# Narrower output products and one copy per four heads in the dilated attention of a decoder trunk

## The chip, the cores and the metric

The kernel runs on one core of one Trainium2 chip. The metric is the device time of one execution in microseconds (us), median of several runs. In the rows, PE is TensorE's matrix multiplication and PEld its weight load, DVE is VectorE, ACT is ScalarE, SP is SyncE; a name with q behind it (ACTq, PEldq) is that engine's queue or sequencer.

## The reference, cut to what matters

The program is one step of a two-layer trunk: a gated DeltaNet layer with its MLP, then a dilated attention layer with its MLP, for 1,024 prompt tokens and 8 sample tokens. The change touches the attention of the prompt tokens alone:

```python
HEADS_B = 8; KV_HEADS_B = 2; GQA_B = 4; HEAD_DIM_B = 64; N_BRANCH = 3
...
        kg = jnp.take(k_ext, kidx, axis=1).astype(jnp.float32)
        vg = jnp.take(v_ext, kidx, axis=1).astype(jnp.float32)
        s = jnp.einsum('nqhgd,nqkhd->nqhgk', q_blk.astype(jnp.float32), kg) * scale + bias
...
        p = jnp.exp(s - lse)
        o = jnp.einsum('nqhgk,nqkhd->nqhgd', p, vg)
```

Eight query heads share two key/value heads ("groups"), four each; a value row has 64 columns for each group. Three branches (dilations 1, 4 and 16) are computed apart and merged by their softmax denominators. In the einsum for `o`, a head needs the 64 value columns of its own group and no others.

## The kernel before, in words

Each engine has its own hand-written instruction stream; the order of the work is the order of the code in it, and the engines meet through counting semaphores (`bank4_free`, `bank4_full`, `probs_ready`, `out_taken` and so on). After the query and key/value projections and the attention of the samples come the 24 prompt tiles: three branches of 8 tiles of 128 queries. `tiles_of` (line 375) walks the tiles on every engine and calls that engine's `step(cur, nxt)`, so the scores of the next tile are made between the parts of the current one. A tile sees nk = 1 or 2 blocks of 128 keys: branch 0 has one tile with nk = 1 and seven with nk = 2; branch 1 has nk = 1 and nk = 2 by turns; branch 2 has nk = 1 throughout. A tile's eight heads are worked in two halves (hs = 0 and 1).

- PE, `step` at line 2170: `turn(cur, 0)` transposes the probabilities of four heads into bank 4 and 5 (line 1770, in `transposes`); `scores(nxt)` makes the next tile's scores in banks 0 to 3 (L2142); then `turn(cur, 1)`, `apply(cur, 0)`, `apply(cur, 1)`. `apply` is the output product (L2165): for each of four heads and each key block, the weights are the transposed probabilities (128x128, f32) and the moving operand is the key block's 128 value columns, both groups. So a head's result takes 128 columns of bank 6 or 7, and half of them, those of the other group, are never read.
- DVE, `step`: `turned` copies transposed probabilities from bank 5 to SBUF (L1630), `biased` adds the bias to the scores (L1612), `maxima` takes the row maxima (L1619, L1622), and `outputs` (L1634 to 1644) copies the softmax statistics and then, for each half, the wanted 64 columns of each head into `o_out`: one copy for each group of a half, 128x128 elements each, four in a tile.
- ACT, `step`: the exponentials (L848), the copy of bank 4 when nk = 2 (L862), and, behind `out_taken`, two DMA issues that store the tile's `o_out` (L881).

In the f32 products here each `matmul` of the code shows as two records in the trace, each with its own weight load. The 560 records of L2165 are 280 products: 8 for each of 13 tiles with nk = 1, and 16 for each of 11 with nk = 2. After the tiles the branches are merged (DVE L1698, L1704), and the output projection and the last MLP follow, long streams of matmuls at L1743 to L1745.

Of the kernel before, what the change touches and what calls it, by code (L numbers as in the profile page):

```python
# [23 lines left out]
P = 128  # L24
# [12 lines left out]
HD = 64  # L37
# [51 lines left out]
        "relu_square_ready": 12, "u_hi_ready": 12},  # L89
# [85 lines left out]
def build(nc, t):  # L175
# [4 lines left out]
    def sem(name):  # L180
        if name not in made:
            made[name] = ctx.enter_context(nc.semaphore(name))
        return made[name]
# [3 lines left out]
    def at(name, shape, dt, where=None, word=4):  # L187

        size = int(np.prod(shape[1:])) * word
        if where is None:  # L190
            place = offset[0]
            offset[0] += -(-size // 32) * 32
        else:
            place = where[0]
            where[0] += -(-size // 32) * 32
            assert where[0] <= where[1], (name, where)
        return nc.alloc_sbuf_tensor_at(name, list(shape), dt, offset=place)
# [101 lines left out]
    v_keys = at("v_keys", [P, BRANCH, CH, P], F32, a)  # L299
    q_tile = at("q_tile", [P, 2, 4, P], F32, a)  # L300
    prob = at("prob", [P, 2, 8, 2 * P], F32, a)
    prob_t = at("prob_t", [P, 2, 8, P], F32, a)
    bias = at("bias", [P, 8, 2 * P], F32, a)
    o_out = at("o_out", [P, 2, OW], F32, a)
# [23 lines left out]
    psum = ctx.enter_context(nc.psum_tensor("psum", [P, 8, HALF], F32))  # L328
# [574 lines left out]
    def _(dve):  # L903
        L = Lane(dve, sem, room=["out0_stored", "out1_stored", "head_output_stored", "state_stored"])
        v = dve
# [608 lines left out]
        def attention_layer():  # L1514
            stored = [0, 0]
            for gi in range(5):
# [4 lines left out]
                for n in range(3 * tiles):  # L1521
# [5 lines left out]
                    third, tile = divmod(n, tiles)  # L1527
                    b = gi - 2 if gi > 1 else 2 * gi + tile // 2
                    d = DIL[b]
                    w = prompt_width(third)  # L1530

                    def by_class(ap):

                        return ap.rearrange("p (r i) -> p i r", r=d)[:, prompt(third, d)]
                    bank = psum[:, TAKES[n % 6]]
                    src = bank[:, 0:w].rearrange("p (i r) -> p i r", r=d)
                    scale = rs[:, prompt(third)].rearrange("p (i r) -> p i r", r=d)
                    mark = "dve_order" if third == 2 else "product_free"
                    v.wait_ge(sem("product_full"), L.next("product_full"))
                    if gi < 2 and tile % 2 == 0:  # L1540
                        for g in range(2):
                            rows = slice(g * HD, (g + 1) * HD)
                            done = v.tensor_tensor(by_class(k_mask[rows, b, g]), src[rows], scale[rows], ALU.mult)
# [89 lines left out]
            def outputs(par):  # L1633

                v.wait_ge(sem(f"out{par}_stored"), L.next(f"out{par}_stored", 32))
                v.tensor_copy(o_out[:, par, 8 * HD:], stats[:, par].rearrange("p m s -> p (m s)")
                ).then_inc(sem("dve_order"), L.add("dve_order"))
                for hs in range(2):
                    v.wait_ge(sem(f"bank{6 + hs}_full"), L.next(f"bank{6 + hs}_full"))
                    for g in range(2):  # L1640
                        dst = o_out[:, par, 0:8 * HD].rearrange("p (g j d) -> p g j d", g=2, j=4)[:, g, 2 * hs:2 * hs + 2]
                        src = psum[:, 6 + hs].rearrange("p (j g c) -> p g j c", g=2, c=P)[:, g, :, g * HD:(g + 1) * HD]
                        mark = ("bank6_free", "out_taken")[hs] if g else "dve_order"
                        v.tensor_copy(dst, src).then_inc(sem(mark), L.add(mark))

            def step(cur, nxt):
                if nxt and (cur is None or nxt[0] != cur[0]):
                    bias_of(nxt[0])
                if cur:
                    turned(cur[3], 0)  # L1650
                if nxt:
                    v.wait_ge(sem(L.last), L.value(L.last))
                    biased(nxt, 0)
                    maxima(nxt, 0)
                    biased(nxt, 1)
                if cur:
                    turned(cur[3], 1)
                if nxt:
                    maxima(nxt, 1)
                if cur:  # L1660
                    outputs(cur[2])
# [10 lines left out]
            for b in range(BRANCH):  # L1672
                mark = "share_args_ready" if b == 2 else "dve_order"
# [16 lines left out]
            with L.loop(CH // 2, "dve merge") as i:  # L1690
                for par in range(2):
# [3 lines left out]
                    for b in range(BRANCH):  # L1695
                        w = share[:, 3, bass.ds(2 * i + par, 1), b].rearrange("p u (j g) -> p (u j) g", g=2)
                        mark = "merge_free" if b == 2 else "dve_order"
# [3 lines left out]
                        if b:  # L1701
                            v.wait_ge(sem(L.last), L.value(L.last))
                            mark = "merged_ready" if b == 2 else "dve_order"
# [27 lines left out]
    def _(pe):  # L1731
        L = Lane(pe, sem, room=["product_free", "out_taken"] + [f"bank{b}_free" for b in range(8)])
        mm = nc.tensor.matmul
# [120 lines left out]
        for h in range(2):  # L1854
            pe.wait_ge(sem(f"bank{6 + h}_free"), L.next(f"bank{6 + h}_free"))
            for k in range(KT):
                done = mm(psum[0:2 * HEADS, 6 + h], w_ab[:, k], x[:, k, halves[h]], start=k == 0, stop=k == KT - 1)
# [3 lines left out]
        for k in range(KT):  # L1861
            done = mm(psum[0:2 * HEADS, 5, 0:NS], w_ab[:, k], s_x[:, k], start=k == 0, stop=k == KT - 1)
# [225 lines left out]
        def attention_layer():  # L2088
            for gi in range(5):
# [3 lines left out]
                for n in range(3 * tiles):  # L2093
                    third, tile = divmod(n, tiles)
# [11 lines left out]
            for b in range(BRANCH):  # L2106
                done = mm(psum[0:NS, 4, b * P:(b + 1) * P], s_kv[:, 2 * b + 1], ident[:], start=True, stop=True)
# [3 lines left out]
            for n in range(NS):  # L2111
# [3 lines left out]
                for b, first, last in ((0, 0, SA), (1, SA, SA + 65), (2, SA + 65, SA + 82), (0, SA + 82, SK)):  # L2115
                    done = mm(psum[0:8, k, lo + first:lo + last], s_qz[:, b, n], s_keys[:, n, first:last],
                              start=True, stop=True)
# [3 lines left out]
            for bank, first, last in ((4, 0, SA), (5, SA, SK)):  # L2121
                pe.wait_ge(sem("bank5_free" if bank == 5 else "s_vrow_ready"), L.next("bank5_free" if bank == 5 else "s_vrow_ready"))
                for n in range(NS):
                    done = nc.tensor.transpose(psum[0:last - first, bank, 8 * n:8 * n + 8], s_p[:, n, first:last],
                                               ident[0:8, 0:8])
# [5 lines left out]
            for n in range(NS):  # L2131
                mm(psum[:, 6, 8 * n:8 * n + 8], s_va[:, n], s_pt[:, 0, 8 * n:8 * n + 8], start=True, stop=False)
                done = mm(psum[:, 6, 8 * n:8 * n + 8], s_vb[:, n], s_pt[0:SB, 1, 8 * n:8 * n + 8], start=False, stop=True)
# [20 lines left out]
            def apply(tile_, hs):  # L2154

                b, tile, par, nk, _ = tile_
                for kt in range(2 - nk, 2):
                    if hs == 1:
                        pe.wait_ge(sem(f"bank{4 + kt}_free"), L.next(f"bank{4 + kt}_free"))
                        L.skip(f"bank{4 + kt}_free", -1)  # L2160
                free = ("bank6_free", "out_taken")[hs]
                pe.wait_ge(sem(free), L.next(free))
                for n in range(4):
                    for kt in range(2 - nk, 2):
                        done = mm(psum[:, 6 + hs, n * P:(n + 1) * P], prob_t[:, kt, 4 * hs + n],  # L2165
                                  v_keys[:, b, bass.ds(tile + kt - 1, 1)].rearrange("p u n -> p (u n)"),
                                  start=kt == 2 - nk, stop=kt == 1)
                done.then_inc(sem(f"bank{6 + hs}_full"), L.add(f"bank{6 + hs}_full"))

            def step(cur, nxt):  # L2170
                if cur:
                    turn(cur, 0)
                if nxt:
                    scores(nxt)
                if cur:
                    turn(cur, 1)
                    apply(cur, 0)
                    apply(cur, 1)
# [150 lines left out]
```

## Time and profile before

| | |
|---|---|
| median of 3 runs | 3120.02 us (3119.8 to 3121.54) |
| the profiled execution's own time | 3127.17 us |
| its span, first to last instruction | 3125.2 us |
| mean granted TensorE clock | 0.949 of 2.4 GHz |
| PE / PEld / DVE / ACT busy over the span | 91% / 89% / 54% / 27% |
| prompt tiles of the attention | about 2080 to 2272 us from the span's start |
| branch 0 / 1 / 2 among them | 2080 to 2152 / 2152 to 2218 / 2218 to 2272 us |
| merge after them | about 2272 to 2325 us |

The profiled execution took 7.15 us more than the median of the runs, so sums are made against its 3127.17 us and their difference is then carried to 3120.02 us. The span is 1.97 us shorter than the execution's own time. Busy shares are averages over stages with different limits: the projections and MLPs are a solid stream on PE, while in the attention the engines hand work to each other.

### The profile page before, as it was taken

Reading aid. Unit: us, or ns where it says so; the run is one execution under the profiler, and the core shown is the slowest. Engines: PE = TensorE matmul, PEld = TensorE weight load, DVE = VectorE, ACT = ScalarE, POOL = GpSimd, SP = SyncE. Lnnn points to the kernel's source line nnn. Section 1 sums busy time; section 2 is a strip of 40 time slices with the busy share of each in tenths; the row PEclk is TensorE's granted clock in tenths of the full one; section 3 lists DMA queues with packets and bytes.
Section 4 is the critical chain, followed back from the end, with each engine's and each line's share of the span. In section 5 each row is a group of like instructions: output and inputs, shape, how many; then the busy total and the mean of one; then the engine's idle time right before and its main releaser. Section 6 shows DMA issues by size and latency. Waiting matters only on the chain. (4 is left out here: it accounts for less than half of the span.)

```text
span 3125.2 us, 47548 instructions
## 1 busy us (share of the span) xinstructions
PE 2853.7 (91%) x18652; PEld 2779.4 (89%) x18652; DVE 1680.2 (54%) x3140; ACT 858.5 (27%) x1907; POOL 0.2 (0%) x4
## 2 busy tenths in 40 slices
PE   5999999999776999999999999758839999999998
PEld 2999999999746999999999999658739999999997
DVE  4766677766344544444444553247867444444445
ACT  3544444444112311221111321025514111122111
POOL 0000000000000000000000000000000000000000
PEclk8999999999757999999999999869969999999999
DMA  3100111102113111111111113731231111111111
GB/s 112 55 17 28 29 35 36 36 16 82 61 47 106 41 54 41 54 40 44 50 40 51 44 55 102 47 90 55 79 117 41 54 41 40 54 40 54 40 41 55
DMA packets 102203, 165.99 MB, mean 53 GB/s; under 512 B 47081, under 2 KB 65809, under 8 KB 101604
## 3 DMA queue, kind: packets, MB, share of 16 engines
q1 hardware_dynamic: 59604, 142.35, 14.3%
q10 hardware_dynamic: 42464, 21.74, 3.5%
q8 instruction: 98, 1.61, 0.2%
q14 instruction: 37, 0.30, 0.0%
HBM read 134.63 MB, written 34.67 MB: 54 GB/s over the span
## 5 line engine op out<-in xcount | busy, mean ns | idle before, releaser
L1743 PE MATMUL psum<-x_hi,w_hi 128*128 128x352 f32 (+1 forms) x2128 | 685.5, 322 | 13.8 <-DVE w_lo L914 7.0
L1744 PE MATMUL psum<-x_lo,w_hi 128*128 128x352 f32 (+1 forms) x2128 | 680.9, 320 | 0.0
L1745 PE MATMUL psum<-x_hi,w_lo 128*128 128x352 f32 (+1 forms) x2128 | 677.7, 318 | 0.0
L1743 PE MATMUL psum<-u_hi,w_hi 128*128 128x352 f32 (+1 forms) x1632 | 524.8, 322 | 2.4 <-DVE u_lo L1717 2.4
L1744 PE MATMUL psum<-u_lo,w_hi 128*128 128x352 f32 (+1 forms) x1632 | 522.2, 320 | 0.0
L1745 PE MATMUL psum<-u_hi,w_lo 128*128 128x352 f32 (+1 forms) x1632 | 520.6, 319 | 0.0
L1743 PEld LDWEIGHTS psum<-x_hi,w_hi 128*128 128x128 f32 x2128 | 400.3, 188 | 17.8 <-DVE x L1432 8.7
L1744 PEld LDWEIGHTS psum<-x_lo,w_hi 128*128 128x128 f32 x2128 | 400.9, 188 | 0.7
L1745 PEld LDWEIGHTS psum<-x_hi,w_lo 128*128 128x128 f32 x2128 | 400.5, 188 | 0.0
L776 ACT ACTIVATE u_hi<-relu 128x352 fp32r<-128x352 f32 (+1 forms) x192 | 94.4, 492 | 1044.1 <-DVE relu L1463 1044.1
L1432 DVE TENSOR_TENSOR x<-x,psum 128x352 f32<-128x352 f32 x336 | 170.6, 511 | 363.7 <-PE psum L1745 363.7
L500 ACT ACTIVATE w_hi<-w_raw,gains 128x512 fp32r<-128x512 f32 x384 | 249.2, 712 | 241.0 <-DMA w_raw<-in_w 132.4
L1743 PEld LDWEIGHTS psum<-u_hi,w_hi 128*128 128x128 f32 x1632 | 307.2, 188 | 3.2 <-issue 2.8
L1744 PEld LDWEIGHTS psum<-u_lo,w_hi 128*128 128x128 f32 x1632 | 307.7, 189 | 0.4
L1745 PEld LDWEIGHTS psum<-u_hi,w_lo 128*128 128x128 f32 x1632 | 307.0, 188 | 0.0
L914 DVE SCALAR_TENSOR_TENSOR w_lo<-w_raw,gains,w_hi 128x512 fp32r<-128x512 f32 x384 | 263.9, 745 | 39.5 <-ACT w_hi L500 39.2
L1845 PE MATMUL psum<-x_hi,w_hi 128*128 128x352 f32 (+1 forms) x768 | 273.0, 355 | 12.8 <-issue 10.3
L1846 PE MATMUL psum<-x_lo,w_hi 128*128 128x352 f32 (+1 forms) x768 | 247.7, 323 | 0.0
L1847 PE MATMUL psum<-x_hi,w_lo 128*128 128x352 f32 (+1 forms) x768 | 247.2, 322 | 0.0
L1460 DVE SCALAR_TENSOR_TENSOR relu<-psum,rs 128x352 f32<-128x352 f32 (+1 forms) x192 | 99.1, 516 | 221.6 <-PE psum L1745 216.8
L1845 PEld LDWEIGHTS psum<-x_hi,w_hi 128*128 128x128 f32 x768 | 147.4, 192 | 13.2 <-issue 10.3
L1466 DVE TENSOR_TENSOR u_lo<-relu,u_hi 128x352 fp32r<-128x352 f32 (+1 forms) x192 | 99.2, 517 | 107.1 <-ACT u_hi L776 107.1
(296 smaller groups left out, 3539.1 us busy)
## 6 DMA issues: line engine op xcount, KB each, us to landing
w_raw<-in_w SPq DMA_DIRECT2D x192, 512.0 KB, 3.7
scratch_att<-o_out ACTq DMA_DIRECT2D x48, 132.0 KB, 2.6
q_tile<-scratch_q SPq DMA_DIRECT2D x24, 256.0 KB, 3.0
merge<-scratch_att SPq DMA_DIRECT2D x8, 768.0 KB, 4.7
scratch_q<-q_stage ACTq DMA_DIRECT2D x24, 176.0 KB, 2.2
x<-in_x SPq DMA_DIRECT2D x8, 516.0 KB, 7.6
scratch_o_heads<-head_out ACTq DMA_DIRECT2D x8, 512.0 KB, 2.7
s_state<-in_s_rec_in ACTq DMA_DIRECT2D x2, 2048.0 KB, 10.0
```

Of the source, the lines that this page charges most:

```text
L500: done = act.activation(w_hi[:, slot, 2 * part + k], w_raw[:, part, k], ACT.Copy, scale=gains[:, bass.ds(unit * UW + 2 * part + k, 1)])
L776: act.activation(u_hi[:, tile, THIRDS[third]], relu[:, 0:width(third)], ACT.Copy).then_inc(sem("u_hi_ready"), L.add("u_hi_ready"))
L914: done = v.scalar_tensor_tensor(w_lo[:, slot, 2 * part + k], w_raw[:, part, k], gains[:, bass.ds(unit * UW + 2 * part + k, 1)], f(w_hi[:, ...
L1432: v.tensor_tensor(out, out, psum[:, TAKES[n % 6], 0:width(third)], ALU.add).then_inc(sem("product_free"), L.add("product_free"))
L1460: v.scalar_tensor_tensor(r, psum[:, TAKES[n % 6], 0:width(third)], 0.0, rs[:, cols], ALU.max, ALU.mult).then_inc(sem("product_free"), L.ad ...
L1466: v.tensor_tensor(u_lo[:, tile, cols], r, f(u_hi[:, tile, cols]), ALU.subtract).then_inc(sem("u_ready"), L.add("u_ready"))
L1743: mm(out, whi, xh[:, k, cols], start=k == 0, stop=False)
L1744: mm(out, whi, xl[:, k, cols], start=False, stop=False)
L1745: done = mm(out, wlo, xh[:, k, cols], start=False, stop=k == kts - 1)
L1845: mm(out, whi, x_hi[:, k, cols], start=k == 0, stop=False)
L1846: mm(out, whi, x_lo[:, k, cols], start=False, stop=False)
L1847: done = mm(out, wlo, x_hi[:, k, cols], start=False, stop=k == KT - 1)
```

## The change

The output product takes only the 64 columns of the head's own group (head 4 hs + n belongs to group n mod 2). Its results stand 64 columns apart, so a half's four heads fill 256 contiguous columns of the bank in the order (j, g, d), and one copy per half of 128x256 elements takes the place of two of 128x128. The semaphore signals of `outputs` stay; the two steps of `dve_order` that marked the first copies go (10 to 6 per loop body in a table of counts, which is otherwise only reordered).

```diff
@@ -1637,11 +1637,10 @@
                 for hs in range(2):
                     v.wait_ge(sem(f"bank{6 + hs}_full"), L.next(f"bank{6 + hs}_full"))
-                    for g in range(2):
-                        dst = o_out[:, par, 0:8 * HD].rearrange("p (g j d) -> p g j d", g=2, j=4)[:, g, 2 * hs:2 * hs + 2]
-                        src = psum[:, 6 + hs].rearrange("p (j g c) -> p g j c", g=2, c=P)[:, g, :, g * HD:(g + 1) * HD]
-                        mark = ("bank6_free", "out_taken")[hs] if g else "dve_order"
-                        v.tensor_copy(dst, src).then_inc(sem(mark), L.add(mark))
+                    dst = o_out[:, par, 0:8 * HD].rearrange("p (g j d) -> p j g d", g=2, j=4)[:, 2 * hs:2 * hs + 2]
+                    src = psum[:, 6 + hs, 0:4 * HD].rearrange("p (j g d) -> p j g d", g=2, d=HD)
+                    mark = ("bank6_free", "out_taken")[hs]
+                    v.tensor_copy(dst, src).then_inc(sem(mark), L.add(mark))
@@ -2162,8 +2161,9 @@
                 for n in range(4):
                     for kt in range(2 - nk, 2):
-                        done = mm(psum[:, 6 + hs, n * P:(n + 1) * P], prob_t[:, kt, 4 * hs + n],
-                                  v_keys[:, b, bass.ds(tile + kt - 1, 1)].rearrange("p u n -> p (u n)"),
+                        cols = slice(n % 2 * HD, (n % 2 + 1) * HD)
+                        done = mm(psum[:, 6 + hs, n * HD:(n + 1) * HD], prob_t[:, kt, 4 * hs + n],
+                                  v_keys[:, b, bass.ds(tile + kt - 1, 1), cols].rearrange("p u n -> p (u n)"),
                                   start=kt == 2 - nk, stop=kt == 1)
```

In the built program one thing is added that the diff doesn't show. On PE, in `apply` for half 0 of a tile inside branch 0's loop (the first of its two steps), a row named ISA computes the address of a value block from the loop's counter. Before:

```order
L2162 REGISTER_ALU
L2165 ISA
L2165 MATMUL psum<-v_keys,prob_t 128x128
L2165 REGISTER_ALU
L2165 MATMUL psum<-v_keys,prob_t 128x128 x7
L2159 REGISTER_ALU x2
```

And now, in the same place:

```order
L2161 REGISTER_ALU
L2165 ISA
L2165 MATMUL psum<-v_keys,prob_t 128x64
L2165 REGISTER_ALU
L2165 MATMUL psum<-v_keys,prob_t 128x64
L2165 ISA
L2165 MATMUL psum<-v_keys,prob_t 128x64
L2165 ISA
L2165 MATMUL psum<-v_keys,prob_t 128x64 x5
L2158 REGISTER_ALU x2
```

Two more address computations stand among the first products. Over the three loop bodies there are 7 such rows more, each run 3 times. Nothing else on PE changes its place, and no weight load is removed.

On DVE, at the end of the same step, the statistics copy and the output copies stand before:

```order
L1635 ISA
L1636 COPY o_out<-stats 128x16
L1639 REGISTER_ALU
L1644 COPY o_out<-psum 128x128 x2
L1639 REGISTER_ALU
L1644 COPY o_out<-psum 128x128 x2
L1630 COPY prob_t<-psum 128x512
```

And now:

```order
L1635 ISA
L1636 COPY o_out<-stats 128x16
L1639 REGISTER_ALU
L1643 COPY o_out<-psum 128x2x2x64
L1639 REGISTER_ALU
L1643 COPY o_out<-psum 128x2x2x64
L1630 COPY prob_t<-psum 128x512
```

Each pair of copies has become one; the waits around them stand as they stood.

## Rows read from the trace of the kernel before

**Rows 1.** The page: busy time by engine over the span.

```profile
PE 2853.7 (91%) x18652; PEld 2779.4 (89%) x18652; DVE 1680.2 (54%) x3140; ACT 858.5 (27%) x1907; POOL 0.2 (0%) x4
```

**Rows 2.** Busy time by stretch: branch 0, branch 1, branch 2.

```profile
core 0: us, PE busy (x) PEld busy (x) DVE busy (x) ACT busy (x) POOL busy (x), PEclk, DMA share, GB/s
2080.00:2152.00 72.00, 63.40 (x429) 57.87 (x427) 56.14 (x112) 38.12 (x138) 0.00 (x0) 0.95 0.17 48
2152.00:2218.00 66.00, 56.42 (x423) 52.20 (x422) 54.02 (x121) 32.74 (x133) 0.00 (x0) 1.00 0.22 65
2218.00:2272.00 54.00, 43.80 (x365) 41.10 (x363) 46.47 (x132) 29.41 (x138) 0.00 (x0) 1.00 0.28 80
```

**Rows 3.** Chain of waits, 2080 to 2272: start, us, what.

```profile
by line: DVE stats L1619 17.1%; PE psum L2165 13.6%; DVE prob L1612 13.2%; ACT prob L848 10.7%; PE psum L2142 10.5%; issue 9.0%; PE psum L1770 7.8%; DVE prob_t L1630 7.6%; ACT prob_t L862 2.5%; DVE neg_max L1622 2.3%; DVE o_out L1644 2.0%; 
...
2120.33 2.05 PE psum L2165 x16
...
2152.17 0.50 DVE o_out L1644 x2
...
2189.85 3.59 PE psum L2165 x32
...
2217.95 0.80 DVE o_out L1644 x4
...
2269.77 1.96 PE psum L2165 x16
```

**Rows 4.** Timeline, weight loads of the output products: start, us, form, count.

```profile
2189.58 3.65 PEld L2165 LDWEIGHTS psum<-v_keys,prob_t 128*128 128x128 f32 x32
...
2241.22 0.97 PEld L2165 LDWEIGHTS psum<-v_keys,prob_t 128*128 128x128 f32 x8
```

**Rows 5.** Timeline, weight loads of other products, 2 and 64 columns wide.

```profile
800.65 27.38 PEld L1982 LDWEIGHTS psum<-s_u,s_state 128*128 128x128 f32 x128 [6.49 <-issue]
...
77.15 0.30 PEld L1879 LDWEIGHTS psum<-ab,ones 128*128 128x128 f32 x2
```

**Rows 6.** The forms of two of those products, and the clock of the stretch.

```profile
L1982 PE MATMUL psum<-s_u,s_state x128: 346/352/353, 800.7 to 827.8; 128*128 128x2 f32 x128
...
L1879 PE MATMUL psum<-ab,ones x2: 275/275/275, 77.2 to 77.3; 128*128 128x64 f32 x2
...
800.00:828.00 28.00, 27.32 (x129) 27.35 (x129) 0.00 (x0) 0.00 (x0) 0.00 (x0) 0.50 0.01 1
76.00:78.00 2.00, 1.59 (x12) 1.45 (x11) 0.56 (x3) 0.00 (x0) 0.00 (x0) 1.00 0.00 0
```

**Rows 7.** Line L2165: its register operations, duration in ns min/median/max.

```profile
L2165 PE MATMUL psum<-v_keys,prob_t x560: 275/275/377, 2089.4 to 2271.4; 128*128 x144, 128*128 128x128 f32 x43
L2165 PEldq FUSED_REGOPS  x15: 46/51/79, 2096.0 to 2257.8; - x15
```

**Rows 8.** Timeline, DVE: pairs and fours of output copies, and a pair of 128x256.

```profile
2120.81 0.49 DVE L1644 COPY o_out<-psum 128x128 f32<-128x128 f32 x2
...
2240.12 0.76 DVE L1612 TENSOR_TENSOR prob<-psum,bias 128x256 f32<-128x256 f32 x2
...
2249.50 0.90 DVE L1644 COPY o_out<-psum 128x128 f32<-128x128 f32 x4
```

**Rows 9.** Two DVE lines, ns min/median/max: a plain copy; 64-element runs.

```profile
L1630 DVE COPY prob_t<-psum x48: 677/681/693, 2084.8 to 2269.8; 128x512 f32<-128x512 f32 x48
...
L1698 DVE TENSOR_TENSOR part<-merge,share x16: 683/688/692, 2283.5 to 2320.9; 128x512 f32<-128x512 f32 x16
```

**Rows 10.** Granted clock behind a PE gap in the DeltaNet stage.

```profile
316.00:318.00 2.00, 2.00 (x10) 0.50 0.00 0
...
314.27 2.08 PE L1952 MATMUL psum<-pair 128*128 128x128 f32 x11 [2.20 <-DVE pair L1291]
```

**Rows 11.** Waits of PE in the attention: us in total, times, longest us.

```profile
PE psum L2165 <- ACT prob_t L862: 6.2, 8, 1.4
```

**Rows 12.** One loop pass of branch 2, two tiles.

```profile
2237.99:2249.86 11.87, 9.62 (x81) 9.07 (x80) 10.60 (x31) 6.59 (x33) 0.00 (x0) 1.00 0.31 90
```

12 rows, old and new, of the table PER are left out of this document.

## The prediction, written before the changed kernel ran

> **What bounds the kernel now.** I read the page's busy times first: PE is busy for 91% of the span and DVE for 54% [rows 1]. That average comes from the projections and MLPs, which the change leaves alone, so the next view is busy time by stretch. In the three branches of prompt tiles nothing is full: PE is busy for 63.40 of 72, 56.42 of 66 and 43.80 of 54 us, DVE for 56.14, 54.02 and 46.47, at a granted clock of 1.00 nearly throughout [rows 2]. So the chain of waits decides. Over the 192 us of the tiles it gives 13.6% to the output products (L2165), 2.0% to the output copies (L1644), and the rest to statistics, biased scores, exponentials, score products, transposes and issue [rows 3]. The reader is to see two things: the whole of what the change touches is 15.6% of 192 us, 30 us, or under 1% of the time; and the products stand on the chain in only some tiles, as 16 or 32 records in a row, while the copies stand there where a branch ends or DVE is the late one.
>
> Behind the tiles the chain runs straight on through the last store into the merge, so a microsecond saved at their end is saved in full.
>
> **What a product costs.** The question is what sets the distance between two records, because each record is a weight load of 128 columns and a pass of the moving operand, and only the second is halved. Today 32 weight loads take 3.65 us; the last takes 0.19, so the distance is (3.65 - 0.19) / 31 = 0.1116 us, and 8 take 0.97 us, (0.97 - 0.19) / 7 = 0.1114 [rows 4]. (0.19 is 0.192, the median load of L2165.) Two rows show the same weight load with less behind it. The sample stage has 128 records that move 2 columns at the clock's lower level, 1.2 GHz: 27.38 us, less the last load's 0.33, over 127 is 0.213 us, which at 2.4 GHz is 0.1065 [rows 5, 6]. And a pair that moves 64 columns at a granted clock of 1.00 takes 0.30 us, a distance of 0.30 - 0.19 = 0.11 [rows 5, 6]. So with 2 columns or 64 the distance is about that of the weight load (a pair's two-digit times leave 0.01 open), and at 128 the two limits nearly coincide. I take 0.1065 for the narrowed products, a saving of 0.0051 us for each record. Bounds: nothing (the 64-column pair), and 0.1116 / 2 = 0.056 if the moving columns alone set the distance.
>
> TensorE: Matmul & The Clock Gate of the Trainium skill has a rule for each side. Its section "LDWEIGHTS (loading the stationary operand)" makes a load's time columns / 1.2, 107 ns for 128 columns whatever is multiplied, and the trace's 0.1065 agrees. Its section "Back-to-back issue gap" gives an isolated gap of N / 2.4 + 2.5 ns, and says itself that pairs of load and matmul are paced by both. By the gap formula alone the sum would be some 11 us of gain; by the load's rule it is 1.
>
> **The sum, part by part.**
>
> - Output products. The chain holds them as one piece of 8 records, seven of 16 and three of 32 (three are in rows 3), 216 of the 560 records. 216 x 0.0051 = 1.1 us saved. The other 344 lie beside work of DVE and ACT and save nothing. Bounds 0 and 216 x 0.056 = 12 us.
> - End of a group. Where DVE waits for the last product, its stream is 64 columns shorter. At two passes' cycles a column (0.1065 us for 128) that is 0.053 us; it counts twice, ahead of the copies at 2152 and at 2271.7: 0.1 us. Bounds 0 and 0.2.
> - Output copies. A plain 128x128 copy takes 0.28 us, a 128x512 one 0.681 [rows 8, 9]; between them, 128x256 is 0.28 + (0.681 - 0.28) / 3 = 0.41. A DVE operation of that size already runs here: a pair of 128x256 takes 0.76 us [rows 8]. So a half's pair goes from 0.49 to 0.41, and four in a row from 0.90 to about 0.75. The new output has runs of 64 elements at three strides. L1698, whose operands have the same 64-long runs, takes 0.688 for 512, as the plain copy does [rows 9], so I charge nothing for it. The chain has the copies in seven places, two of which are in rows 3: fours or most of four at 2217.95, 2244 and 2256, the pairs at 2152.17 and 2271.75, and one pair's worth at each of 2227 and 2232. 3 x 0.14 + 4 x 0.08 = 0.7 us saved. If instead a 256-element copy cost as much as a 512-element one, each pair would lose 0.20 us: seven places, ten pairs, 2.0 us lost.
> - What hides the rest of the copies: of 48 pairs only those ten are on the chain. Elsewhere DVE is waiting for a product or for the next transposes, and a faster copy gives a longer wait. `out_taken` comes earlier for ACT, whose DMA issues stand behind exponentials it has to run anyway.
> - Register operations. Seven more rows, each run three times: 21 operations of 0.051 us [rows 7]. Groups that hold one today keep the same 0.1114 distance as those without [rows 4], so the queue ahead covers it. Without cover (branch 1's three groups of 32 on the chain, and branch 0's first products behind a wait) I count 0.2 us lost. Bounds 0 and 21 x 0.051 = 1.1.
> - Fewer DVE signals (two `dve_order` steps less a tile): nobody waits for them. PSUM banks 6 and 7 come free a little earlier, for products that don't wait for them on the chain. Nothing.
>
> Sum: 1.1 + 0.1 + 0.7 - 0.2 = 1.7 us saved. Against the profiled execution's own 3127.17 us that is 3125.5; carried to the median of the runs, 3120.02 - 1.7 = **3118.3 us**. A measurement of this kernel can tell about 0.2%, 6.2 us, from no change, so the forecast is "within 0.2%".
>
> **The rivals.**
>
> *Moving columns set the pace.* If the load hides wholly behind the previous product, the distance falls to 0.056 and the chain's 216 records save up to 12 us, of which I let a quarter be taken back by what is late next (DVE, at 46.47 of 54 us in branch 2 [rows 2]): 9 and the copies' 0.6, so 3110.4 us, faster by 0.3%. For it: today's distance is also what 128 columns at two cycles each would give, 0.1067, so the trace's main products can't tell the two limits apart. Against it: the 2- and 64-column rows, and their weights are the same 128x128 f32 [rows 5, 6]. It is the gap formula above, of the Trainium skill's page TensorE: Matmul & The Clock Gate, taken alone. It passes 0.2% once the distance is under 0.077: (6.2 - 0.6) / 0.75 / 216 = 0.035 less than today. Chance 0.09.
>
> *The clock falls.* Slower than before. PE has fewer columns to stream for as many loads, and the granted clock might go to its lower level in branch 2, where PE has most idle time. What the trace has for it: 27.32 us of PE busy on 2-column records in a 28 us stretch went at 0.50 from end to end [rows 6], so a busy PE with narrow work did not bring the clock up. Price: a loop pass of two tiles in branch 2 is 11.87 us and has 80 weight loads [rows 12]. At half clock 80 x 0.213 = 17.0 us, so PE becomes the bound and each pass of two tiles is 5.2 us longer; four passes, 21 us, 3139 us. It decides from 8 us of loss on, some three tiles at the low level. Against it: the falls seen elsewhere came behind a PE gap of 2.20 us [rows 10], the attention's longest wait is 1.4 us [rows 11], and the transposes and score products keep their 128 and 256 columns. Chance 0.04.
>
> *The copy is dearer than two.* The 2.0 us of its bound, with 1.1 for the register operations and nothing saved on PE, gives 3123.1 us: still within 0.2%. Chance 0.08.
>
> **How the numbers follow.** Forecast 0.79, rivals 0.09, 0.04 and 0.08. Faster by over 0.2% (below 3113.8) is the first rival less its small versions, and a rest of the forecast for couplings that pay more than the chain shows: 0.08. Slower by over 0.2% (above 3126.3) is the clock: 0.04. Within: 0.88. The range runs from 3113.5, half of what the pace rival gives, to 3121.5, where the dearer copy is half true.
>
> **What would show it.** The records of L2165 still 560, with a distance of 0.106 to 0.111 us (32 loads in 3.5 to 3.65 us); 48 copies in place of 96, each about 0.41 us; the three branches 72, 66 and 54 us long within 1 us each; clock 1.00 in them. A distance near 0.06, or a clock below 0.9 in branch 1 or 2, would make the prediction wrong; so would a copy of 0.6 us or more, in its sign.

## The result, and the profile after

| | before | changed |
|---|---|---|
| median of 15 runs each | 3120.07 us | 3128.61 us |
| lowest to highest | 3117.54 to 3123.45 | 3122.95 to 3136.01 |
| profiled execution's own time | 3127.17 us | 3128.61 us |
| span | 3125.2 us | 3126.8 us |
| mean granted clock over the span | 0.949 | 0.945 |

The ratio of the runs is 1.0024, 95% interval 1.0016 to 1.0032: slower by 0.24%, or 7.5 us; the two medians lie 8.5 us apart. The prediction was 3118.3 us and "within 0.2%", and the time lies above its range (3113.5 to 3121.5). The first profile of the kernel before was an execution 7 us above its own median, so that the two spans differ by only 1.6 us. A comparison of stages needs the tiles alone, and more than one profile; both follow.

The page of the changed kernel, busy time by engine over the span, beside [rows 1]:

```profile
PE 2861.3 (92%) x18652; PEld 2787.2 (89%) x18652; DVE 1678.3 (54%) x3092; ACT 858.0 (27%) x1907; POOL 0.2 (0%) x4
```

DVE has 48 instructions fewer and 1.9 us less to do; PE has the same number of records, no fewer, and 7.6 us more.

Busy time by stretch (us; PE, PEld, DVE, ACT and POOL busy with their counts; granted clock, DMA share, GB/s), the same three as in [rows 2]:

```profile
2080.00:2152.00 72.00, 66.19 (x426) 60.44 (x425) 52.70 (x92) 35.74 (x126) 0.00 (x0) 0.92 0.17 48
2152.00:2218.00 66.00, 57.56 (x413) 53.85 (x412) 52.04 (x102) 32.03 (x128) 0.00 (x0) 0.95 0.22 65
2218.00:2272.00 54.00, 45.69 (x363) 43.78 (x362) 45.76 (x114) 29.41 (x138) 0.00 (x0) 0.94 0.28 80
```

This is where the forecast fell. The clock column reads 0.92, 0.95 and 0.94; before it was 0.95 (its first 7 us only, ahead of the first output product; the changed kernel has 5 such us there), 1.00 and 1.00 [rows 2]. PE is busier in every branch for fewer streamed columns, DVE idler. Two microseconds at a time, one of the places looks like this (PE alone):

```profile
core 0: us, PE busy (x), PEclk, DMA share, GB/s
2104.00:2106.00 2.00, 1.33 (x13) 1.00 0.00 0
2106.00:2108.00 2.00, 1.59 (x15) 1.00 0.00 0
2108.00:2110.00 2.00, 1.79 (x9) 0.66 0.29 64
2110.00:2112.00 2.00, 2.00 (x6) 0.50 0.76 202
2112.00:2114.00 2.00, 2.00 (x10) 0.98 0.00 0
```

PE had small pauses (1.33 and 1.59 busy of 2 us), and within 2108 to 2110 the granted clock went from its upper level, 2.4 GHz, to its lower, 1.2 GHz; some 3 us later it was back. A DMA burst begins at the same time, but it isn't the cause: the same bursts at 2090 and 2100 us (share 0.83 and 0.79 of 2 us) bring no fall, and the next fall, at 2118, has no DMA beside it (share 0.00). The pauses alone aren't it either, for the kernel before has larger ones at a clock of 1.00 (columns as above):

```profile
2236.00:2238.00 2.00, 1.15 (x8) 1.00 0.00 0
2238.00:2240.00 2.00, 1.39 (x14) 1.00 0.06 16
```

The chain of waits of the changed kernel around it (start, us, what):

```profile
2108.20 1.57 PE psum L1769 x8
2109.78 2.94 PE psum L2141 x8
...
2117.70 2.61 PE psum L2165 x16
2120.31 1.71 PE psum L1769 x8
2122.01 1.95 PE psum L2141 x8
```

The same pieces of the kernel before:

```profile
2112.51 1.09 PE psum L1770 x8
2113.60 1.74 PE psum L2142 x8
...
2120.33 2.05 PE psum L2165 x16
2122.37 0.87 PE psum L1770 x8
2123.25 1.74 PE psum L2142 x8
```

Eight score records that took 1.74 us take 2.94, eight transposes 1.57 in place of 1.09, and a little later 16 output records 2.61 in place of 2.05 and eight transposes 1.71 in place of 0.87. These four pieces are 1.2 + 0.5 + 0.6 + 0.8 = 3.1 us longer, over two falls (2108 to 2112 and 2118 to 2122 us), which is more than the whole change was to save.

The terms of the sum have their rows too. Weight loads of the output products, branch 1 (timeline), beside [rows 4]:

```profile
2190.50 3.66 PEld L2165 LDWEIGHTS psum<-v_keys,prob_t 128*128 128x128 f32 x32
```

(3.66 - 0.19) / 31 is 0.112 us: the distance has not moved. The lines of the changed products and of the merged copy (count, ns min/median/max), beside [rows 7] and [rows 9]:

```profile
L2165 PE MATMUL psum<-v_keys,prob_t x560: 221/275/427, 2086.1 to 2272.7; 128*128 x144, 128*128 128x64 f32 x43
L2165 PEldq FUSED_REGOPS  x36: 46/46/79, 2091.7 to 2259.4; - x36
```

```profile
L1643 DVE COPY o_out<-psum x48: 412/424/425, 2088.6 to 2273.2; 128x256 f32<-128x256 f32 x48
```

The shortest product record is 221 ns where it was 275, 0.054 us less; register operations went from 15 to 36; a merged copy takes 0.424 us. The longest wait of PE for the transposed probabilities (us in total, times, longest), beside [rows 11]:

```profile
PE psum L2165 <- ACT prob_t L862: 6.6, 8, 1.5
```

### The profile page after: what moved, and what is told of

Read it like the earlier page. It is cut to its first block and busy times, and to the rows that moved or that the text cites. A ratio compares the mean times of both kernels' runs of the same rounds, so it can differ in the third digit from the quotient of the medians.

```text
span 3126.8 us, 47521 instructions
## 1 busy us (share of the span) xinstructions
PE 2861.3 (92%) x18652; PEld 2787.2 (89%) x18652; DVE 1678.3 (54%) x3092; ACT 858.0 (27%) x1907; POOL 0.2 (0%) x4
```

## The experiments

Theory A: the narrow products leave the granted clock to fall in part of the tiles, whatever the tiles save otherwise. Theory C: the merged copy costs. Theory R: the 21 added register operations cost. Diffs are against the changed kernel; those of the two later filler kernels are against the first of them. Each timed kernel ran in 5 rounds beside the kernel before on the same chip. For each, the fence gives PE by branch (stretches of 62, 66 and 47 us: busy, count, granted clock, DMA share, GB/s); the kernel before has a clock of 1.00 in all three, the changed kernel 0.94, 0.95 and 0.93.

### One copy, wide products

```diff
-                    src = psum[:, 6 + hs, 0:4 * HD].rearrange("p (j g d) -> p j g d", g=2, d=HD)
+                    src = psum[:, 6 + hs].rearrange("p (j g c) -> p j g c", g=2, c=P)[:, :, :, 0:HD]
+                    src = bass.AP(src.tensor, src.offset, [[192, 2] if i == 2 else list(x) for i, x in enumerate(src.ap)])
...
-                        done = mm(psum[:, 6 + hs, n * HD:(n + 1) * HD], prob_t[:, kt, 4 * hs + n],
-                                  v_keys[:, b, bass.ds(tile + kt - 1, 1), cols].rearrange("p u n -> p (u n)"),
+                        done = mm(psum[:, 6 + hs, n * P:(n + 1) * P], prob_t[:, kt, 4 * hs + n],
+                                  v_keys[:, b, bass.ds(tile + kt - 1, 1)].rearrange("p u n -> p (u n)"),
```

> Products as before, 128 columns wide; only the copy is changed (one operation of 128x256 for each half, reading 64-column runs out of the wide results). Theory A (the narrow products take streamed columns away and the granted clock falls in part of the tiles): clock 1.00 in all three branches from 2090 us on, time 0.3 to 2 us under before, about 3119 us. Theory C (the merged copy is what costs): about 3127 us, at a clock of 1.00. Theory R (the 21 added register operations of the narrow products cost): as A, about 3119.

Measured: 3120.52 us beside 3121.56 (ratio 0.9996, 0.9987 to 1.0005).

```profile
2090.00:2152.00 62.00, 56.55 (x405) 1.00 0.20 59
2152.00:2218.00 66.00, 57.35 (x431) 1.00 0.22 65
2218.00:2265.00 47.00, 38.11 (x318) 1.00 0.28 80
```

```profile
L1644 DVE COPY o_out<-psum x48: 414/425/426, 2088.0 to 2265.6; 128x256 f32<-128x256 f32 x48
```

The clock is whole and the loss gone. The merged copy takes 0.425 us here as well. Theory C falls. In the one profile the tiles, from the first output record to the last, take 180.7 us where they took 182.0, so the copy is worth 1.3 us there; the runs can't tell that from nothing.

### Narrow products, two copies

The changed kernel with the two copies of each half put back:

```diff
+                    for g in range(2):
...
+                        src = psum[:, 6 + hs, 0:4 * HD].rearrange("p (j g d) -> p g j d", g=2, d=HD)[:, g]
```

> Products 64 columns wide, but two copies of 128x128 for each half as before. Theory A: stretches at the clock's lower level in the tiles as in the changed kernel (mean 0.92 to 0.96 by branch), time 3127 to 3131 us. Theory C: back to 3118 to 3120 us. Theory R: 3127 to 3131 us, and most of the loss at full clock.

Measured: 3132.35 us beside 3121.56 (1.0037, 1.0023 to 1.0051).

```profile
2090.00:2152.00 62.00, 56.42 (x388) 0.94 0.17 47
2152.00:2218.00 66.00, 56.88 (x405) 0.95 0.21 62
2218.00:2265.00 47.00, 39.64 (x306) 0.91 0.28 81
```

The narrow products alone bring the whole loss, and the low stretches with it. It came out a little above the 3131 us expected of it.

### 32 columns

```diff
-                        cols = slice(n % 2 * HD, (n % 2 + 1) * HD)
-                        done = mm(psum[:, 6 + hs, n * HD:(n + 1) * HD], prob_t[:, kt, 4 * hs + n],
+                        cols = slice(n % 2 * HD, n % 2 * HD + 32)
+                        done = mm(psum[:, 6 + hs, n * HD:n * HD + 32], prob_t[:, kt, 4 * hs + n],
```

> The changed kernel with only 32 of the 64 value columns of each head multiplied; the other 32 results are left out, so its output is not the reference's. Loads, register operations and copies as in the changed kernel. Theory A: less work and yet slower than the changed kernel, since more stretches fall to the lower level: mean clock under 0.92 over the tiles, 3132 to 3150 us. Theories R and C: 3127 to 3129 us, as the changed kernel.

Measured: 3142.75 us beside 3121.56 (1.0065, 1.0051 to 1.0079).

```profile
2090.00:2152.00 62.00, 57.34 (x324) 0.78 0.16 43
2152.00:2218.00 66.00, 59.44 (x388) 0.86 0.20 57
2218.00:2265.00 47.00, 41.55 (x308) 0.90 0.27 80
```

Half the columns of the changed kernel (the other 32 results of each head are left out), everything else the same, and 21.2 us over the kernel before where the changed kernel is 8.5 over it: less work, more time. Neither theory C nor R has a way to that.

### A filler of 256 columns

```diff
-                for kt in range(2 - nk, 2):
-                    if hs == 1:
-                        pe.wait_ge(sem(f"bank{4 + kt}_free"), L.next(f"bank{4 + kt}_free"))
-                        L.skip(f"bank{4 + kt}_free", -1)
                 free = ("bank6_free", "out_taken")[hs]
                 pe.wait_ge(sem(free), L.next(free))
+                if hs == 1:
+                    mm(psum[:, 7, 256:512], prob_t[:, 1, 3], k_mask[:, 0, 0, 0:256], start=True, stop=True)
+                for kt in range(2 - nk, 2):
+                    if hs == 1:
+                        pe.wait_ge(sem(f"bank{4 + kt}_free"), L.next(f"bank{4 + kt}_free"))
+                        L.skip(f"bank{4 + kt}_free", -1)
```

> The changed kernel with one more f32 product of 256 columns for each tile, into unused columns of bank 7, where PE waits for the second half's transposed probabilities (0.8 us idle in branch 0 loops); its result is never read. It takes about 0.44 us, and restores 256 of the 512 (nk = 1) or 1,024 (nk = 2) columns removed per tile. Theory A: the lower level goes or becomes rare, time 3117 to 3122 us, faster than the changed kernel though it does more. Theory R or C: no gain, 3128 to 3135 us.

Measured: 3121.37 us beside 3121.56 (1.0000, 0.9991 to 1.0009).

```profile
2090.00:2152.00 62.00, 59.74 (x427) 1.00 0.20 59
2152.00:2218.00 66.00, 59.69 (x413) 0.95 0.20 59
2218.00:2265.00 47.00, 42.10 (x341) 1.00 0.28 83
```

The narrow products and all 21 register operations are in it, and 48 more records, and it is 0.24% faster against the kernel before than the change without them. So theory R falls as well. One stretch at the lower level is left, where branch 0 goes over into branch 1 and DVE makes a new bias table.

### A filler of two columns

```diff
-                    mm(psum[:, 7, 256:512], prob_t[:, 1, 3], k_mask[:, 0, 0, 0:256], start=True, stop=True)
+                    for at_ in (256, 258):
+                        mm(psum[:, 7, at_:at_ + 2], prob_t[:, 1, 3], k_mask[:, 0, 0, 0:2], start=True, stop=True)
```

> As the kernel with the filler, but the filler's 256 columns are replaced by two products of 2 columns: four weight loads in place of two, about 0.45 us of PE at the same place, hardly any column streamed. If it is streamed columns that hold the clock (theory A): the lower level stays in the tiles (mean 0.92 to 0.96) and the time is 3127 to 3133 us. If it is PE's share of busy time (theory A2): as with the filler, 3119 to 3123 us and clock 1.00 in branches 0 and 2.

Measured: 3129.93 us beside 3121.64 (1.0023, 1.0012 to 1.0033).

```profile
2090.00:2152.00 62.00, 59.68 (x392) 0.89 0.16 48
2152.00:2218.00 66.00, 59.39 (x428) 0.95 0.22 65
2218.00:2265.00 47.00, 42.87 (x346) 0.93 0.27 80
```

This is the sharpest pair of the study. In branch 0 the two kernels with fillers keep PE busy for the same time, 59.74 and 59.68 of 62 us, with the filler in the same place; the one that streams 256 columns is granted 1.00, the one that streams four 0.89. Part of that busy time is itself the low clock's, which makes records longer, so the time ahead of a fall tells more (the kernel with the thin filler, columns as above):

```profile
2104.00:2106.00 2.00, 1.82 (x17) 1.00 0.00 0
2106.00:2108.00 2.00, 1.39 (x8) 0.60 0.00 0
```

From 2102 to 2106 us PE was busy for 3.82 of 4 us at full clock, and then the clock fell, with no pause above 0.6 us beside it; it was so ahead of the falls at 2126 and 2140 us too. The kernel before had 2.54 of 4 us from 2236 to 2240 us, and no fall. So PE's share of busy time doesn't hold the clock here. A filler with next to no columns gave nothing back.

### 96 columns

The products take the head's own 64 columns and 32 of the other group; the copy's strides follow.

```diff
-                        cols = slice(n % 2 * HD, (n % 2 + 1) * HD)
-                        done = mm(psum[:, 6 + hs, n * HD:(n + 1) * HD], prob_t[:, kt, 4 * hs + n],
+                        cols = slice(n % 2 * 32, n % 2 * 32 + 96)
+                        done = mm(psum[:, 6 + hs, n * 96:(n + 1) * 96], prob_t[:, kt, 4 * hs + n],
```

> Products 96 columns wide (the head's own 64 and 32 of the other group), one copy for each half, register operations as in the changed kernel. Theory A: between the two widths, nearer the wide one: clock 0.97 to 1.00 over the tiles, time 3119 to 3124 us. Theory R (register operations): 3127 to 3130 us, as the changed kernel has.

Measured: 3120.38 us beside 3121.64 (0.9999, 0.9990 to 1.0008).

```profile
2090.00:2152.00 62.00, 55.54 (x407) 1.00 0.18 52
2152.00:2218.00 66.00, 56.99 (x416) 0.97 0.22 65
2218.00:2265.00 47.00, 39.66 (x312) 0.94 0.28 80
```

As the clock theory has it for the time. The clock in branch 2, 0.94, is under the 0.97 expected: there were low stretches, though fewer.

### Narrow in branch 0 alone

```diff
+                        if b == 0:
+                            dst, src = slice(n * HD, (n + 1) * HD), v_keys[:, b, bass.ds(tile + kt - 1, 1), n % 2 * HD:(n % 2 + 1) * HD]
+                        else:
+                            dst, src = slice(n * P, (n + 1) * P), v_keys[:, b, bass.ds(tile + kt - 1, 1)]
+                        done = mm(psum[:, 6 + hs, dst], prob_t[:, kt, 4 * hs + n], src.rearrange("p u n -> p (u n)"),
```

The copy takes its source by branch in the same way.

> Products 64 columns wide in branch 0 alone and 128 wide in branches 1 and 2; one copy for each half everywhere. Theory A: clock below 1.00 in branch 0 only, 1.00 in the two others, about half of the loss (the records of branch 0 are 232 of 560): 3121 to 3127 us. Theory R: 3 of 7 register rows remain, about the same time, at full clock.

Measured: 3126.45 us beside 3121.64 (1.0017, 1.0008 to 1.0026).

```profile
2090.00:2152.00 62.00, 56.48 (x367) 0.90 0.16 46
2152.00:2218.00 66.00, 58.86 (x429) 0.96 0.22 65
2218.00:2265.00 47.00, 38.80 (x326) 1.00 0.29 86
```

The fall stays with the narrow products: 0.90 in branch 0, 1.00 in branch 2. The 0.96 of branch 1 is one stretch from 2149 to 2157 us, at the end of branch 0, that carries over the border of the windows. (By count the records of branch 0 are 7 x 32 + 16 = 240, not 232; the forecast of half the loss stands with it.)

### More filler

```diff
-                    mm(psum[:, 7, 256:512], prob_t[:, 1, 3], k_mask[:, 0, 0, 0:256], start=True, stop=True)
+                    for _ in range(2 if b == 1 and nk == 1 else 1):
+                        mm(psum[:, 7, 256:512], prob_t[:, 1, 3], k_mask[:, 0, 0, 0:256], start=True, stop=True)
```

> As the kernel with the filler, with a second filler in the tiles of branch 1 that see one key block, where its profile still had one stretch at the lower level. Theory A: no stretch below 1.00 from 2090 us on, but 4 x 0.44 us more PE time: 3118 to 3121 us, the same as before within the error. A version that beats both would show 3117 us or less.

Measured: 3119.08 us beside 3121.64 (ratio of the paired runs 0.9998, 0.9989 to 1.0007).

```profile
2090.00:2152.00 62.00, 58.84 (x421) 1.00 0.18 52
2152.00:2218.00 66.00, 61.43 (x454) 1.00 0.22 67
2218.00:2265.00 47.00, 39.65 (x302) 0.92 0.30 83
```

The fall at the start of branch 1 is gone. Against expectation one stands in the last tile of branch 2; 3.4 us of that window also lie behind the last product, at 2261.6. No version beat both kernels by more than the runs can tell.

### Both kernels profiled again

The changed kernel and the kernel before, unedited, twice each, one execution a profile.

> The changed kernel, profiled once more, since the first profile's tiles are only 4.6 us longer than before where the medians differ by 8.5. Theory A: from the first output product to the last 186 to 195 us, another set of stretches at the lower level, 15 to 35 us of them; the stages behind the last product the same 854 us to the end. If part of the loss lies elsewhere, that part shows outside these.

> The kernel before, profiled once more. Theory A: 181 to 183 us from the first output product to the last, clock 1.00 throughout them, 854 us behind.

> The changed kernel, a third profile: as for the second, with the low stretches in other places again (theory A: they aren't tied to one tile).

> The kernel before, a third profile: 181 to 183 us, clock 1.00, 854 us behind. A low stretch in the tiles here would mean that the kernel before is at the edge too.

Measured, one time each: 3135.15 and 3129.06 us for the changed kernel, 3121.55 and 3120.33 us for the kernel before. The changed kernel, second profile:

```profile
2090.00:2152.00 62.00, 57.45 (x353) 0.86 0.18 51
2152.00:2218.00 66.00, 58.67 (x414) 0.92 0.22 64
2218.00:2265.00 47.00, 40.41 (x302) 0.89 0.24 71
```

The kernel before, second profile:

```profile
2090.00:2152.00 62.00, 56.40 (x408) 1.00 0.19 55
2152.00:2218.00 66.00, 56.55 (x424) 1.00 0.22 65
2218.00:2265.00 47.00, 37.67 (x313) 1.00 0.29 80
```

All profiles side by side. "Tiles" is from the start of the first L2165 record (or its line in that kernel) to the start of the last. "Low" is the time at the lower level, worked out from the three clock figures as 2 x (1 - clock) x length, summed, since the lower level is half. The three stretches end at 2265 us; where the tiles run on, a fall behind that isn't in the column (counted to the last product, 32 columns has 58 us and the filler of 2 columns 31).

| profile | tiles, us | low, us | behind the last product, us |
|---|---|---|---|
| before, three profiles | 182.0, 182.0, 182.0 | 0, 0, 0 | 853.8, 853.9, 853.9 |
| changed, three profiles | 186.6, 193.8, 189.5 | 21, 38, 31 | 854.1, 854.6, 853.9 |
| one copy, wide products | 180.7 | 0 | 853.8 |
| narrow, two copies | 189.3 | 23 | 854.2 |
| 32 columns | 201.8 | 55 | 854.1 |
| filler of 256 columns | 183.3 | 7 | 854.7 |
| filler of 2 columns | 192.9 | 27 | 853.9 |
| 96 columns | 183.3 | 10 | 854.0 |
| narrow in branch 0 alone | 186.0 | 18 | 854.8 |
| more filler | 182.3 | 4 (8 less 3.4 behind the tiles) | 854.7 |

That closes the account. The mean of the changed kernel's three profiles is 190.0 us, 8.0 above the kernel before, beside 8.5 at the medians; what lies behind the tiles is the same to a microsecond. What lies ahead of them isn't touched: the first product starts at 2089.4, 2083.7 and 2082.4 us in the kernel before and at 2086.1, 2084.9 and 2083.9 us in the changed one, and the first of these is the profile that was 7 us long. From the one-copy kernel, which has all but the narrow products, to the changed kernel's mean it is 9.3 us for 30 us at the lower level: 0.3 us lost for each microsecond there (0.28 to 0.34 in the three profiles, 0.36 with 32 columns). If PE alone made up the chain, half of each microsecond there would be lost; only 31.9% of the chain in the tiles is PE's (L2165, L2142 and L1770 in [rows 3]), and by that share it would be 0.319 / 1.319 = 0.24. That the rest is PE work which comes onto the chain at the lower clock is an argument that no run was made for. The low stretches stand mostly in other tiles in each profile, though each of the three has one near the border of branches 0 and 1 (at 2159, 2154 and 2149 us), and the changed kernel's runs spread over 13 us where the kernel before has 6.

## Why the prediction was wrong

- **The step that failed** is the term that the sum put at nothing: it took the granted clock to stay at 1.00 in the tiles ("clock 1.00 in them") and left the clock to a rival with a chance of 0.04. In its place the runs showed 21, 38 and 31 us of the tiles at the lower level, and the tiles 4.6 to 11.8 us longer. The rival rested on "PE has fewer columns to stream for as many loads", and that is what happened. Two arguments were set against it: the falls seen elsewhere came behind a PE gap of 2.20 us [rows 10], and the transposes and score products keep their columns. Both are true, and neither kept the clock up. It fell with no PE wait for the transposed probabilities above 1.5 us (1.4 before), and, with the thin filler, right behind 3.82 busy of 4 us. The row that spoke for the rival, 27.32 us of busy PE at 0.50 on 2-column records [rows 6], was read rightly and weighed too low.
- **Its place and price.** I put it in branch 2 throughout, 21 us. It came in all three branches, for some 3 to 7 us at a time, 21 to 38 us an execution. By the measured 0.3 us for each microsecond that is 6 to 12 us. The price was about right: the prediction has 5.2 us lost for a pass of 17.0 us at the lower level, also 0.3 for each microsecond. How much of the stretch would be low was not something the rows of before could say, as they show no fall in the tiles behind the first.
- **Output products, 1.1 us.** Mis-sized, and the distance between loads gave nothing: 32 loads take 3.66 us, not 3.5. The pace is that of the weight load, as I argued, but at the upper level it is 0.1116 us and not half of the 0.213 seen at the lower. The 64-column pair's 0.11, which I had as the bound of no gain, was the better row. The rival in which moving columns set the pace is excluded: with 32 columns too, eight loads take 0.97 us and 32 take 3.65, as before. Where no fall comes, the change does pay a little: in branch 1 the second and third groups of 32 on the chain start 16.10 and 16.28 us behind the one ahead of them in the kernel before, 15.97 and 15.99 us with one copy and wide products, 15.93 and 15.92 us in the changed kernel.
- **The Trainium skill's two rules.** In TensorE: Matmul & The Clock Gate, section "LDWEIGHTS (loading the stationary operand)", the load's time goes by its own columns alone. At the upper level the trace agrees: the distance is 0.112 us with 32, 64 and 128 moving columns, beside the 0.107 that the formula gives for a load of 128 (an estimate). The agreement claimed in the prediction was with 0.1065, a figure halved from the lower level, where the distance itself is 0.213 us. The isolated gap formula of "Back-to-back issue gap" did not describe this stream of pairs.
- **End of a group**, 0.053 us each: the record got 0.054 shorter (27 ns for each 32 columns, by shortest records of 275, 248, 221 and 194 ns at 128, 96, 64 and 32 columns). Right, and by the sum worth 0.1 us in all, which the runs can't show.
- **Output copies.** 0.41 us a copy predicted, 0.424 measured; 0.7 us saved predicted, 1.3 us in the one profile of the one-copy kernel. Right in kind; where the other 0.6 us came from wasn't taken apart.
- **The dearer copy**, a rival with 0.08, is excluded: 0.424 us a copy, and no loss in the kernel that has it without the narrow products.
- **Register operations.** 21 more, as counted. The kernels with the filler and with 96 columns have them too and lose nothing measurable, so nothing contradicts the 0.2 us; the runs, good to some 3 us, can't confirm it.
- **The range and the test.** The lower end, 3113.5 us, isn't half of what the pace rival gives (3120.02 - 9.6 / 2 is 3115.2); this didn't decide anything. The test "a clock below 0.9 in branch 1 or 2" was set as the sign of error; the first profile had 0.95 and 0.94. A sign of 1.00 against 0.95 would have been the right one, since one stretch of 3 us costs 1 us or more, by the price above, and two undo what was forecast.

What stays open: why a given tile falls in one execution and not in the next. No run here tells it.

## What to carry to other kernels

This is one kernel, but its questions can be asked of any trace. Before taking columns from matmuls in a stage that waits a lot, ask two things of the trace: whether the distance between records follows the moving columns at all (here it followed the weight load, so there was nothing to gain), and whether the granted clock is still whole where PE streams less. Where the chain saves a microsecond or two and PE gets markedly less to stream, the clock is the first rival and not the last; its price is read from rows at either level and multiplied by a few stretches. The safe part of such a change, here the merged copy, can often be had alone by letting the reader pick its runs out of a wide result.

## What the runs showed that I had not expected

Useless columns carried the clock: 64 columns a head that nobody reads kept it at 1.00 for 180 us, and a product whose result nobody reads gave most of it back (3121.37 us beside 3129.93 for one in the same place that streams four columns). Taking away half of the remaining columns made the loss 21.2 us in place of 8.5. And f32 weight loads of 128 columns, each with its product, follow each other at a distance of 0.1116 us at 2.4 GHz beside 0.213 at 1.2 GHz, a ratio of 1.91 and not 2.
